# Moving two projection units of a hybrid decoder step: one across a barrier, one past a wait

## What is computed

```
h = rmsnorm(x) * (1 + sc1) + sh1
hq, hf, hi, hg, fq, fk, fv, ff, mg = split(h @ w_in)
o_h = rmsnorm(hgrn_chunked(q, k, v, log f)) * silu(hg);  br_h = o_h @ w_br_h
br_f = fox_attend(fq, cached and new keys and values, log-forget sums) @ w_br_f
g_h, g_f = split(sigmoid(mg))
y = (g_h * br_h + g_f * br_f) @ w_out
```

## Time and profile before

| | |
|---|---|
| median of three runs | 2052.27 us (2043.08 to 2056.32) |
| the profiled execution, as a run | 2048.03 us |
| its span from first to last instruction | 2046.4 us |
| PE busy | 1915.2 us, 94% of the span |
| DVE, ACT, POOL busy | 697.3, 599.4, 391.5 us |
| granted clock of PE, mean over the span | 0.98 |

### The profile page before, as it was taken

The page is one execution under the profiler, slowest core; times in us unless marked ns, Lnnn a source line. Parts: engine busy times, 40 slices in busy tenths (PEclk is TensorE's granted clock), DMA queues, the critical chain, the costliest instruction groups (busy, mean ns, idle before and its releaser), DMA issues.

```text
span 2046.4 us, 32380 instructions
## 1 busy us (share of the span) xinstructions
PE 1915.2 (94%) x12832; PEld 1621.9 (79%) x12832; DVE 697.3 (34%) x899; ACT 599.4 (29%) x869; POOL 391.5 (19%) x427
## 2 busy tenths in 40 slices
PE   4988989689899998999999999999999999999996
PEld 2777867567788897777777778999999999999976
DVE  3634243454444443112111464232223121322235
ACT  5545344332333332011101332322222222222221
POOL 2222021222111111101000062213030303021203
PEclk9999999899999999999999999999999999999998
DMA  8111011487121122323322532111111111111132
GB/s 285 32 33 43 22 34 41 128 298 250 52 53 42 31 63 74 103 83 96 95 77 63 151 124 63 57 42 51 42 41 41 47 45 41 41 42 50 42 118 88
DMA packets 137680, 159.88 MB, mean 78 GB/s; under 512 B 10697, under 2 KB 111354, under 8 KB 136442
## 3 DMA queue, kind: packets, MB, share of 16 engines
q1 hardware_dynamic: 119568, 104.94, 16.7%
q0 software_dynamic: 15776, 46.68, 7.5%
q10 hardware_dynamic: 2250, 7.04, 1.0%
HBM read 142.72 MB, written 15.91 MB: 78 GB/s over the span
## 4 chain that ended last, share of the span: by engine, by line
PE 83%; DVE 4%; issue 3%; DMA 3%; ACT 3%; SPq 2%; POOLq 1%; POOL 1%; DVEq 1%; ACTq 0%; PEldq 0%; PEld 0%
PE psum L272 42%; PE psum L2219 16%; PE psum L2066 6%; PE psum L2113 4%; PE psum L1807 2%; PE psum L1820 1%; DVE nmax L1304 1%; ACT work L955 1%; PE psum L2168 1%; SPq L449 1%; PE psum L1888 1%; PE psum L1882 1%; PE psum L2040 1%; DMA work<-in_cache_k 1%; DMA work<-in_cache_v 1%
## 5 line engine op out<-in xcount | busy, mean ns | idle before, releaser
L272 PE MATMUL psum<-h_hi,w_hi 128*128 128x288 f32 (+1 forms) x1776 | 401.1, 334 | 11.2 <-POOLq L719 4.1
L272 PE MATMUL psum<-h_lo,w_hi 128*128 128x288 f32 (+1 forms) x1776 | 394.4, 331 | 0.0
L272 PE MATMUL psum<-h_hi,w_lo 128*128 128x288 f32 (+1 forms) x1776 | 394.2, 330 | 0.0
L272 PEld LDWEIGHTS psum<-h_hi,w_hi 128*128 128x128 f32 x1776 | 269.8, 189 | 48.8 <-issue 18.8
L260 DVE TENSOR_TENSOR w_lo<-w_raw,w_hi 128x1024 fp32r<-128x1024 f32 x108 | 165.6, 1533 | 380.4 <-ACT w_hi L254 373.2
L272 PEld LDWEIGHTS psum<-h_lo,w_hi 128*128 128x128 f32 x1776 | 270.2, 189 | 28.6
L272 PEld LDWEIGHTS psum<-h_hi,w_lo 128*128 128x128 f32 x1776 | 270.1, 188 | 28.6
L822 POOL TENSOR_TENSOR work<-work 128x1088 f32<-128x1088 f32 x56 | 142.5, 2545 | 512.9 <-ACTq L1144 512.9
L2219 PE MATMUL psum<-u_hi,w_lo 128*128 128x288 f32 (+1 forms) x672 | 148.4, 328 | 0.0
L2219 PE MATMUL psum<-u_lo,w_hi 128*128 128x288 f32 (+1 forms) x672 | 148.4, 328 | 0.0
L2219 PE MATMUL psum<-u_hi,w_hi 128*128 128x288 f32 (+1 forms) x672 | 148.3, 328 | 0.0
(11 more groups left out here) (367 smaller groups left out, 2339.6 us busy)
## 6 DMA issues: line engine op xcount, KB each, us to landing
w_raw<-in_w_in SPq DMA_DIRECT2D x44, 512.0 KB, 3.8
work<-in_cache_k SPq DMA_DIRECT2D x64, 256.0 KB, 5.6
work<-in_cache_v POOLq DMA_DIRECT2D x64, 256.0 KB, 4.8
work<-in_ada_w POOLq DMA_DIRECT2D x32, 512.0 KB, 4.0
w_raw<-in_w_mlp_up SPq DMA_DIRECT2D x32, 512.0 KB, 4.0
w_raw<-in_w_mlp_down SPq DMA_DIRECT2D x32, 512.0 KB, 3.4
work<-in_ada_w SPq DMA_DIRECT2D x8, 1024.0 KB, 16.4
out<-work POOLq DMA_DIRECT2D x12, 512.0 KB, 4.0
```

What stands on the lines that cost most here:

```text
L272: last = nc.tensor.matmul(out[:, a:b], w, m[:, k, a:b], start=(k == 0 and w is wh and m is h_hi), stop=(k == KD - 1 and w is wl))
```

## The change

Three things are changed, all in the order or the waits of PE, with one place of DVE that follows.

1. PE runs unit 14 (`U_HG + 1`, the queries of head 0) right after it has signalled its end of phase 3, ahead of its wait for the other engines' signals. Head 0 then starts with unit 15; it is written out ahead of the loop, which now runs over heads 1 and 2.
2. Since unit 14 writes the banks 0 to 2, the last sample's output transpose goes to bank 6 (`output_columns`, `mixed`).
3. The second gate unit of the first block (unit 30) waits for one reading fewer of the accumulators, that is, no longer for ACT's sigmoid of unit 29.

```diff
 # DVE
-            def mixed(b):
+            def mixed(b, src=bank(2, 2 * P, 3 * P)):
...
-                        bank(2, 2 * P, 3 * P)[64 * i:64 * i + 64, :].rearrange("p (g c) -> p g c", c=32)
+                        src[64 * i:64 * i + 64, :].rearrange("p (g c) -> p g c", c=32)
...
-            mixed(NB - 1)
+            mixed(NB - 1, src=bank(6, 0, P))
 # PE
-            def output_columns(b):
+            def output_columns(b, out=bank(2, 2 * P, 3 * P)):
...
-                tr(bank(2, 2 * P, 3 * P), sO, ident[:, :]).then_inc(so_tr, 1)
+                tr(out, sO, ident[:, :]).then_inc(so_tr, 1)
...
-            output_columns(NB - 1)
-            phase_end(pe, "pe", 3)
+            output_columns(NB - 1, out=bank(6, 0, P))
+            pe.drain().then_inc(done_of["pe"], 1)
+            project(pe, U_HG + 1, (U_HG + 1) % 2)
+            for e in ("act", "dve", "pool"):
+                pe.wait_ge(done_of[e], 3)
 
             pe.wait_ge(hg_zeroed, 1)
-            def head(h):
-                for j in range(1, 4):
+            def head(h, first=False):
+                for j in range(2 if first else 1, 4):
                     n, slot, _ = number(U_HG, 4, h, j)
                     project(pe, n, slot)
...
-            with pe.Fori(0, HH - 1) as h:
+            head(0, first=True)
+            with pe.Fori(1, HH - 1) as h:
                 head(h)
             head(HH - 1)
...
-                    def gate(j, pairs=True):
+                    def gate(j, pairs=True, unread=0):
...
-                        pe.wait_ge(acc_read, n)
+                        pe.wait_ge(acc_read, n - unread)
...
                     if first_pair and dd == 0:
-                        gate(1, pairs=False)
+                        gate(1, pairs=False, unread=1)
```

## The result

The changed kernel takes 2037.55 us at the median of 19 runs, the kernel before 2048.61 us at the median of 19 runs beside it. The ratio is 0.9941, with a 95% interval from 0.9928 to 0.9954: about 12 us less, 9 to 15. One run of each kernel took far longer than the rest (2995.20 us before, 4745.41 us the change), and the ratio leaves both out. Run again beside other kernels, the ratio was 0.9955 (0.9936 to 0.9975), about 9 us less. The forecast of 2043 us had the direction, and its range held the time; its gain of 7.2 us was too small. The prediction held that a measurement tells only about 20 us from no change; this one tells 9.

A forecast was written before the change was run, and what follows sets the result against it. The prediction took TensorE (PE), busy for 94% of the span, as the bound. Gains of 4.9 and 2.3 us made 7.2 us, taken from the middle execution's 2050.15 us to forecast 2043 us, range 2035 to 2052.

The forecast's parts named there:

- Unit 14 ahead of the barrier: At the barrier ending sample attention: unit 14 starts 3.3 us earlier and loses no clock (1.6 us), gaining 4.9 us.
- given back: Rival, head 0: a ScalarE or VectorE step hangs on the barrier, losing the first gain; gain 2.3, 2047.9 us, chance 0.12.
- Second gate unit: At the gate: starts without waiting for the sigmoid, gain cut by landing modulation weights to 2.3 us, 5.1 without that wait.
- the new wait: Behind the second gate unit: PE waits for two modulation weight pieces to land, 2.0 and 0.8 us.
- The sum: Whole kernel: 4.9 us at the barrier plus 2.3 us at the gate, 7.2 us gained.
- The head stretch: Heads behind unit 14: they move as a whole, with no wait between units 14 and 15.
- The clock falls in the new wait: Rival, behind the modulation weight wait: PE drops to the low clock, costing 1.4; gain 5.8, 2044.4 us, chance 0.18.
- Slower by instruction fetch: Rival, PE's longer program: about 4 more packets on 62, up to 15 us of stalls, 8 us slower, 2058, chance 0.06.

The follow-up runs named there:

- filled_barrier: Kernel before plus 14 unread matmuls on PE between its signal for barrier 3 and its wait for the other engines; profiled once, 2038.88 us.
- unit14_only: Edits 1 and 2 alone: unit 14 ahead of the barrier wait, second gate unit again behind the sigmoid; ratio to the kernel before 0.9962.
- head0_out: Kernel before with head 0 written out ahead of the loop and nothing else, unit 14 still behind the barrier; ratio 0.9995.
- after_again: The changed kernel, unaltered, run and profiled once more beside other kernels; ratio to the kernel before 0.9955.
- gate_only: Kernel before with only the second gate unit's wait for the first gate unit's sigmoid removed; ratio 0.9976.
- late_requests: Changed kernel with six more memsets and drains on POOL ahead of its modulation weight requests; profiled once, 2038.74 us.
- requests_first: Changed kernel with POOL's first two modulation weight requests ahead of its branch weight requests; ratio to the kernel before 0.9946.
- filled_heads: Changed kernel with POOL's memset, copy and first two modulation requests moved earlier, plus seven unread matmuls per head; ratio to before 0.9916, median 2030.02 us.
- after: First profile of the changed kernel against the kernel before; that profiled execution took 2033.32 us as a run.

## Why the prediction was right, and where its size was off

*Unit 14 ahead of the barrier, 4.9 us.* Right. Unit 14 ends 14.32 to 14.49 us after the first mark in every kernel that has the edit, 19.17 to 19.59 without it (`filled_barrier` left out): 4.7 to 5.3 us. The split into 3.3 us of start and 1.6 us of clock holds by `filled_barrier`. No wait arose between units 14 and 15, and the rival "given back" falls.

*Second gate unit, 2.3 us.* The mechanism was right, the term too small. Without the edit the branch starts 18.65, 19.37, 20.21 and 19.49 us after the transposes (before, `unit14_only`, `head0_out`, `filled_barrier`), 19.43 on average; with it 15.20, 15.28 and 15.63, 15.37 on average. That is 4.1 us. Two things were mis-sized. The first is what is taken away: 18.7 us was the lowest of four, since the clock loss behind the sigmoid's wait was 1.3 us there and up to 2.9 elsewhere (15.12 - 12.23). The second is the new wait: 2.0 and 0.8 us were expected, 0.89 and 0.47 came in the first profile (1.28 and 0.48, 1.48 and 0.47 in `after_again` and `gate_only`), since POOL's requests went out 0.7 us sooner and PE's unit ended later, its sigmoid starting at 803.44 or 12.7 us after the transposes in place of 12.4. `late_requests` and `requests_first` show that the landing is what limits the branch.

*The sum.* 4.9 and 4.1 make 9.0 us in place of 7.2. The head stretch, which the forecast left at nothing, was 1.6 us shorter in the first profile and 3.0 in the second; that is scatter rather than the change, since the heads take 264.6 to 269.2 us in the four profiles without the early unit and 264.3 to 268.7 in the seven with it (`filled_heads` left out), and their length goes with the granted clock in all twelve. The rest up to the measured 12 us, with an interval that begins at 9.4, is not resolved by these runs. The forecast of 2043 also stood 1.5 us high at its start, taken from the middle of four executions (2050.15) where 19 runs gave 2048.61.

*The clock falls in the new wait.* Half right as a rival: not in `after` and `gate_only`, but in `after_again`, whose first 4 us of the branch were granted 0.57 on average, and in `late_requests`. The window, wait and chain of `after_again`:

```profile
807.00:811.00 4.00, 4.00 (x12) 2.40 (x9) 0.00 (x0) 0.00 (x0) 0.73 (x2) 0.57 0.78 249
```

```profile
PE psum L2044 <- DMA work<-in_ada_w: 1.8, 2, 1.3
```

```profile
807.10 9.19 PE psum L2070 x24
```

The 24 matmuls took 7.51 us in `after`, so the low clock cost 1.7 us there, about what the prediction put to this rival (1.4). That the first profile shows none of it is luck as much as foresight: behind the longer first wait of `gate_only` (1.48 us against 1.28) the clock held. The prediction took this cost as nothing because the clock held behind one wait of 2.04 us. It left out four waits of 1.7 to 1.9 us in the heads of the same profile, each followed by the low clock (shown above), so the rival deserved more than its 0.18. The Trainium skill (TensorE: Matmul & The Clock Gate, "HAM oscillation — how this bites in real kernels") describes it for bursts of matmuls that are shorter than the waits for data between them. In these profiles the clock falls behind some waits of this length and not behind others, and what decides it stays open.

*Slower by instruction fetch.* The count was right: 66 packets in place of 62. They cost nothing that any profile shows.

## What to carry to other kernels

An idle stretch of the engine that bounds the kernel costs its length and can cost the low clock behind it: here always behind the two waits of 4 us, and in 30 of 44 cases behind waits of 1.7 to 1.9 us. One profile shows only one outcome of the second part, so such a term is better read from several profiles, and from every wait of like length in them, or given as a range (here 1.3 to 2.9 us behind the sigmoid's wait). Before work is pulled ahead over a wait, look for the transfers that were hidden under the old wait: here a request made behind a barrier became the next bound, and moving the request was a change of a few lines.

## What was not expected of the hardware

A drain on POOL behind several requests took long: 3.4 to 4.2 us for the first one behind four requests and 5.4 us behind six. The drains behind it, with memsets of 0.31 us alone between, let each next memset start 0.43 us after the one before (`late_requests`). Nothing in the program waits for it by name; the profile shows it as a wait for no reason.
